# Where the causal mask is added: VectorE in PSUM instead of a TensorE product with a unit matrix

## The chip, the cores and the metric

The kernel runs on one core of one Trainium2 chip. The metric is the device time of one execution in microseconds (us). Before the change three runs took 1765.3, 1765.32 and 1770.0 us; the median is 1765.32 us. The profile is of a further execution.

## The reference, cut to what matters

One decoder layer is computed for a prompt of 1024 tokens and for 8 sample tokens. The change touches only the prompt's attention, with 8 heads and two softmax maps per head:

```python
s = jnp.einsum('bqhcd,bkhcd->bhcqk', q, k).astype(jnp.float32) * (HEAD_DIM ** -0.5)   # c: the two maps
s = jnp.where(mask[None, None, None], s, NEG_INF)        # causal: key position <= query position
p = jax.nn.softmax(s, axis=-1)
a = p[:, :, 0] - lam * p[:, :, 1]
return jnp.einsum('bhqk,bkhe->bqhe', a.astype(v.dtype), v)
```

Queries come in 8 blocks of 128. Block i needs the keys of blocks 0 to i, and only its last score block, the one on the diagonal, has masked places. The rest of the layer (projections, pooling branch, sample attention, gates, MLP) is as it was.

## The kernel before

All products are float32 values split into a high and a low part, three matmuls for each product (L707, L731, L800, L1035, L1097). The program is one instruction stream per engine, written out by hand, with a semaphore for each hand-over. The stages in order of time are: the normed input and the first projection (to about 65 us), eight heads of attention (65 to 552 us), the pooling and sample branches with their projections (to about 1050 us), and the MLP.

**One head on TensorE.** `head(h, par, proj, normed)` (L806) runs steps s = 0 to 8. A step has, in this order: `scores(h, par, s)` (L719), `values(h, par, s-2)` (L758), the first half of the projection of the next head for token tile s (`project`, L681, the matmuls of L707), `weight_transposes` of query block s-1 (L738, L754), the second half of the projection, and `qk_transposes` of the next head for tile s-1 (L716, L717). The last head has no next one, so nothing is projected in it. In steps 0 to 7 `scores` makes the score rows of one query block for both maps c, in PSUM tensor `bank_s` (two banks for each map), in matmuls that contract over 64 rows (L731). At its end two matmuls (L735), one for each map, multiply a bf16 unit matrix by the bf16 mask, and accumulate it on the diagonal block. Their ends raise the semaphore `s_s`.

**The same head on VectorE** (L1596). A step has `maximum` for map 0 and for map 1 (L1554: a wait for `s_s`, the row maximum L1558, the bias L1561), `o_sum` (L1586), `weight_low` (L1580), `weights` (L1568 to L1573), `rotate` (L1543 to L1547, its last instruction raises `s_zfree`, the leave for the next projection to overwrite its bank) and `qk_low` (L1551). In step 1 `normed_head` stands behind the maxima, with a wait for GpSimd's square root (L2152). ScalarE's step is the two exponentials (L1160, each waits for its bias), then `o_out` (L1173), which `o_sum` waits for, then `weight_high` (L1167), which `weight_low` waits for, then the squares, and the copies of the rotated q, k and v.

**What TensorE waits for in a head.** `scores(s)` waits for the exponentials of step s-1 (`s_exp`), as they read the same banks. `values(s-2)` waits for `weight_low` of that block (`s_atlo`). `project(h+1, s, 0)` waits for an earlier `rotate` (`s_zfree`, with the count of `z_before`, L368): of tile 0 in step 2, of tile s-1 in steps 3 to 7, and in step 0 of tile 8 of the head before. `qk_transposes` waits from tile 4 on for `weight_low` (`s_atlo`).

Of the kernel before, what the change touches and what calls it, by code (L numbers as in the profile page):

```python
# [5 lines left out]
ALU = mybir.AluOpType  # L6
# [4 lines left out]
BF16 = mybir.dt.bfloat16  # L11

P = 128
# [63 lines left out]
def decoder_layer(nc, ins, outs):  # L77
# [18 lines left out]
    def put(name, shape, dtype, at=None):  # L96
        size = 1
        for n in shape[1:]:
            size *= n
        size *= 2 if dtype == BF16 else 4  # L100
        off = cursor[0] if at is None else at
        t = nc.alloc_sbuf_tensor_at(name, shape, dtype, offset=off)
        end = (off + size + 31) // 32 * 32
        if at is None:
            cursor[0] = end
        return t, end

    ident, _ = put("ident", [P, P], F32)
    identb, _ = put("identb", [P, P], BF16)
    mask, _ = put("mask", [P, P], BF16)  # L110
    stat, _ = put("stat", [P, 64], F32)
    cols, _ = put("cols", [P, 32], F32)
    nlam, _ = put("nlam", [P, 1], F32)
    half_neg, _ = put("half_neg", [P, 64], F32)
    ones, _ = put("ones", [P, P], F32)
    pages, _ = put("pages", [1, DEC * PAGES], mybir.dt.int32)
    base_h = cursor[0]
    h_hi, _ = put("h_hi", [P, KT, TOK], F32R)
    h_lo, _ = put("h_lo", [P, KT, TOK], F32R)
    w_raw, _ = put("w_raw", [P, 3, KT, P], F32)  # L120
    w_hi, _ = put("w_hi", [P, 3, KT, P], F32R)
    w_lo, _ = put("w_lo", [P, 3, KT, P], F32R)
# [3 lines left out]
    kv_st, _ = put("kv_st", [P, 2, NTT + 1, 2, P], F32)  # L126
    qs_st, _ = put("qs_st", [P, 2, P], F32)
    q_nat, _ = put("q_nat", [P, P], F32)
    qk_hi, _ = put("qk_hi", [P, 2, 2, SEQ], F32R)
    qk_lo, _ = put("qk_lo", [P, 2, 2, SEQ], F32R)  # L130
    v_hl, _ = put("v_hl", [P, 2, NTT, 2, P], F32R)
    rope_c, _ = put("rope_c", [P, NTT + 1, HD], F32)
    rope_s, _ = put("rope_s", [P, NTT + 1, HD], F32)
    rc, _ = put("rc", [P, 2 * P], F32)
    rs, _ = put("rs", [P, 2 * P], F32)
    sums, _ = put("sums", [P, NTT, 2], F32)
    rsum, _ = put("rsum", [P, NTT, 2], F32)
    mx, _ = put("mx", [P, 2, 2], F32)
    nbias, _ = put("nbias", [P, 2, 2], F32)
    ratio, _ = put("ratio", [P, 2], F32)  # L140
    ssq, _ = put("ssq", [P, 2, NTT], F32)
    o_var, _ = put("o_var", [P, NTT], F32)
    o_rstd, _ = put("o_rstd", [P, NTT], F32)
    junk, _ = put("junk", [P, P], F32)
    o_low, _ = put("o_low", [P, P], F32)
    over = cursor[0]
    prob, _ = put("prob", [P, 2, 2, SEQ], F32)
    aT_hi, _ = put("aT_hi", [P, SEQ], F32R)
    aT_lo, _ = put("aT_lo", [P, SEQ], F32R)
    o_st, _ = put("o_st", [P, 2, NTT, P], F32)  # L150
    oT_st, _ = put("oT_st", [P, SEQ], F32, (nc.sbuf_usable_end - 4 * SEQ) // 32 * 32)
# [8 lines left out]
    mask_in, a = put("mask_in", [P, P], F32, a)  # L160
# [6 lines left out]
    kv_slots, _ = put("kv_pages", [P, 2, HEADS // 2 * TOK], F32, r2)  # L167
    kv_pg = kv_slots[:, :, 0:PAGES * D].rearrange("p s (g d) -> p s g d", g=PAGES)
    o_raw, _ = put("o_raw", [P, HEADS, TOK], F32, r2)
    o_lo, _ = put("o_lo", [P, HEADS, TOK], F32R, r2)  # L170
    x1, _ = put("x1", [P, KT, TOK], F32, r2)
# [7 lines left out]
    merged, _ = put("merged", [P, KT, TOK], F32, r3)  # L179
    gx, _ = put("gx", [P, KT, TOK], F32, r3)  # L180
    ff_lo, a = put("ff_lo", [P, KH, TOK], F32R, r3)
    ff_hi, _ = put("ff_hi", [P, KH, TOK], F32R, a)
    ff_raw, _ = put("ff_raw", [P, KH, TOK], F32, r3)
# [3 lines left out]
    smp_q, _ = put("smp_q", [P, D], F32, tmp)  # L187
    smp_k, _ = put("smp_k", [P, D], F32, r4 - 4 * D)
    smp_v, _ = put("smp_v", [P, D], F32, r4 + 2 * NG * TOK * 4 - 4 * TOK)
    ga_sig, _ = put("ga_sig", [P, KT, TOK], F32, r4)  # L190
    o_hi = nc.alloc_sbuf_tensor_at("o_hi", [P, HEADS, TOK], F32R, offset=base_h + full)
    mg_hi = nc.alloc_sbuf_tensor_at("mg_hi", [P, KT, TOK], F32R, offset=base_h)
    mg_lo, _ = put("mg_lo", [P, KT, TOK], F32R, r4)
# [8 lines left out]
    h_smp, _ = put("h_samples", [P, KT, LOW_ROW + DEC], F32R, a)  # L202
# [6 lines left out]
    z_smp, _ = put("z_smp", [P, 3 * P], F32, a)  # L209
# [14 lines left out]
    x_smp, _ = put("x_smp", [P, D], F32, slot2[0])  # L224
# [4 lines left out]
    sq_sum, _ = put("sq_sum", [P, TOK], F32, tmp)  # L229
    diag, a = put("diag", [P, NTT + 1, P], F32, a)  # L230
    assert a <= nc.sbuf_usable_end
    r_bc, _ = put("r_bc", [P, TOK], F32, tmp)
# [45 lines left out]
    with ExitStack() as ctx:  # L278
# [6 lines left out]
        def sem(name):  # L285
            return ctx.enter_context(nc.semaphore(name))
# [37 lines left out]
                                                                  "sample_exp")]  # L324
        s_sela, s_vout, s_v, s_osq, s_oss, s_osv, s_osr, s_osmp = [sem(n) for n in (
            "sel_weights", "v_out", "v_ready", "os_steps", "os_sum", "os_var", "os_rstd", "os_ready")]
        s_hread = sem("h_low_read")
        s_ohi, s_olo, s_addm, s_mghi, s_mglo = [sem(n) for n in ("o_hi", "o_lo", "merged_added", "mg_hi", "mg_lo")]
        s_xt, s_xc, s_sqr, s_sqs = sem("xT_ready"), sem("xT_out"), sem("x1_squares"), sem("squares_added")
        s_n2, s_v2, s_r2 = [sem(n) for n in ("n2_sum", "n2_var", "n2_rstd")]  # L330
# [337 lines left out]
        def _(pe):  # L668
# [50 lines left out]
            def scores(h, par, i):  # L719

                pe.wait_ge(s_qklo, 8 * h + i + 1)
                need(pe, s_exp, 16 * h + 2 * i)
                if i == 4 and h < HEADS - 1:
                    pe.wait_ge(s_zfree, z_before(h + 1, NTT))
                diag = i // 4
                for b in range(1 + diag):
                    n = min(512, (i + 1) * P - 512 * b)
                    for m, (q, k) in enumerate(((qk_hi, qk_hi), (qk_lo, qk_hi), (qk_hi, qk_lo))):
                        for c in range(2):
                            part = slice(HD * c, HD * c + HD)  # L730
                            pe.matmul(bank_s[:, c, 512 * b:512 * b + n], q[part, par, 0, i * P:(i + 1) * P],  # L731
                                      k[part, par, 1, 512 * b:512 * b + n], start=(m == 0),
                                      stop=(m == 2))
                for c in range(2):
                    pe.matmul(bank_s[:, c, i * P:(i + 1) * P], identb[:], mask[:], start=False, stop=True,  # L735
                              skip_group_check=True).then_inc(s_s, 1)

            def weight_transposes(h, i, r, proj):  # L738

# [118 lines left out]
            for t in range(NTT + 2):  # L858
# [6 lines left out]
                if t >= 2:  # L865
                    need(pe, s_qklo, t - 3)
                    qk_transposes(0, 0, t - 2, bank_t[t % 2])
            pe.wait_ge(s_mask, 1)
            head(0, 0, True, False)
            for p in range(0, HEADS // 2 - 1):  # L870
                head(2 * p + 1, 1, True, True)
# [625 lines left out]
        def _(dve):  # L1497
# [56 lines left out]
            def maximum(h, i, c):  # L1554
                n = (i + 1) * P
                k = 16 * h + 2 * i + c + 1
                dve.wait_ge(s_s, k)
                dve.tensor_reduce(mx[:, i % 2, c:c + 1], bank_s[:, c, 0:n], AX_X, ALU.max).then_inc(s_mx, 1)  # L1558
                dve.wait_ge(s_mx, k)
                need(dve, s_exp, k - 4)  # L1560
                dve.tensor_scalar(nbias[:, i % 2, c:c + 1], mx[:, i % 2, c:c + 1], -SCALE, None,  # L1561
                                  ALU.mult).then_inc(s_nb, 1)
# [33 lines left out]
            def head(h, par, proj, normed, k_par):  # L1596
                if proj:
                    split_qkv(h + 1, (2, 3) if normed else (0, 1, 2, 3))
                for s in range(NTT + 1):
                    if s < NTT:  # L1600
                        maximum(h, s, 0)
                        maximum(h, s, 1)
                    if normed and s == 1:
                        normed_head(h - 1, 1 - par)
                    if s >= 2:
                        o_sum(h, par, s - 2)
                    elif s == 0 and normed:
                        o_sum(h - 1, 1 - par, NTT - 1)
                    if s >= 1:
                        weight_low(h, s - 1, 0)  # L1610
                    if s >= 5:
                        weight_low(h, s - 1, 1)
                    if s < NTT:
                        weights(h, s)
                    if s == NTT and h < HEADS - 2:
                        split_qkv(h + 2, (0, 1))
                    if proj:
                        rotate(h + 1, 1 - par, s, k_par)
                    if proj and s >= 1:
                        qk_low(h + 1, 1 - par, s - 1)  # L1620

            def lambda_steps():

                dve.wait_ge(s_const, N_CONST)
                dve.tensor_copy(mask[:], mask_in[:])
                dve.tensor_copy(identb[:], ident[:]).then_inc(s_mask, 1)
                dve.tensor_tensor(lam_pr[:], lam_in[:, 0:4:2], lam_in[:, 1:4:2], ALU.mult).then_inc(s_lam_pr, 1)
                dve.wait_ge(s_lam_pr, 1)
                dve.tensor_reduce(stat[:, 32:34], lam_pr[:], AX_X, ALU.add).then_inc(s_lam_sum, 1)
# [14 lines left out]
            for t in range(NTT + 5):  # L1644
# [20 lines left out]
                if t == NTT + 3:  # L1665
                    lambda_ready()
            dve.wait_ge(s_lam, 1)
            head(0, 0, True, False, 0)
            for p in range(0, HEADS // 2 - 1):
                head(2 * p + 1, 1, True, True, p + 1)  # L1670
# [562 lines left out]
```

## Time and profile before

| | |
|---|---|
| median of 3 runs | 1765.32 us |
| profiled execution, its own time | 1771.14 us |
| its span, first to last instruction | 1769.1 us |
| TensorE matmul busy | 1713.0 us (97%) |
| VectorE busy | 1057.6 us (60%) |
| ScalarE busy | 671.3 us (38%) |
| mean granted TensorE clock | 0.989 of 2.4 GHz |

The span is cut into engine instructions with their start, duration and operands; L735 is line 735 of the kernel. "Idle before" is time in which the engine did nothing ahead of an instruction, with the instruction on another engine whose end released it. TensorE's matmuls are pipelined: the distance from start to start is what one costs in a stream, and the duration also holds the time to run out.

### The profile page before, as it was taken

What the parts mean: (1) busy time and instruction counts of PE and PEld (TensorE: products, weight loads), DVE (VectorE), ACT (ScalarE), POOL (GpSimd) and SP (SyncE); (2) the same over time, 40 slices, a digit from 0 to 9 for tenths busy, and PEclk for the clock granted to TensorE, in tenths of its full rate; (3) what the DMA queues carried; (4) which work ended last, traced back from release to release, by engine and by line L of the source; (5) the groups of instructions that cost most, each with busy time, mean ns of one, the idle gap of its engine ahead of it and who ended that gap; (6) DMA issues with size and microseconds to landing.
All of it is one profiled execution on the core that took longest, in us unless ns stands there. A gap on an engine that the chain in (4) does not pass through costs nothing.

```text
span 1769.1 us, 29201 instructions
## 1 busy us (share of the span) xinstructions
PE 1713.0 (97%) x11756; PEld 1658.1 (94%) x11756; DVE 1057.6 (60%) x1725; ACT 671.3 (38%) x1417; POOL 136.4 (8%) x244
## 2 busy tenths in 40 slices
PE   6999999999977999999999999999999999999997
PEld 6889889888967999999999999999999999999997
DVE  5677777777764788764344457363636363646454
ACT  4355555555544222354312445141414141314132
POOL 3212221221210000000000000000000000000001
PEclk9999999999979999999999999999999999999999
DMA  6202201220220637575222221111111120202112
GB/s 189 70 2 72 73 26 48 73 61 13 73 65 12 224 107 242 171 242 178 93 60 79 65 73 48 49 49 48 49 48 61 36 72 25 72 26 71 48 37 97
DMA packets 136526, 139.13 MB, mean 79 GB/s; under 512 B 6721, under 2 KB 114177, under 8 KB 136384
## 3 DMA queue, kind: packets, MB, share of 16 engines
q1 hardware_dynamic: 135239, 133.07, 24.4%
q10 hardware_dynamic: 1152, 4.19, 0.6%
q8 instruction: 94, 1.54, 0.4%
q14 instruction: 41, 0.33, 0.1%
HBM read 120.29 MB, written 17.18 MB: 78 GB/s over the span
## 4 chain that ended last, share of the span: by engine, by line
PE 90%; DVE 5%; issue 2%; ACT 2%; DMA 1%; SPq 0%; POOL 0%; DVEq 0%; ACTq 0%
PE ps L800 23%; PE ps L1097 21%; PE ps L1035 18%; PE ps L707 16%; PE ps L731 3%; PE ps L764 3%; PE ps L754 1%; PE ps L935 1%; DVE kv_pages L1739 1%; DMA w_raw<-in_w_in 1%; PE ps L735 1%; DVE w_lo L1502 1%; DVE mx L1558 1%; PE ps L773 0%; DVE y_st L2114 0%
## 5 line engine op out<-in xcount | busy, mean ns | idle before, releaser
L2024 DVE TENSOR_TENSOR x<-ps,x 128x1032 f32<-128x1032 f32 x64 | 78.9, 1233 | 223.4 <-PE ps L1097 223.4
L707 PE MATMUL ps<-w_hi,h_hi 128*128 128x384 f32 x520 | 182.6, 351 | 5.8 <-DVE w_lo L1502 3.7
L707 PE MATMUL ps<-w_hi,h_lo 128*128 128x384 f32 x520 | 177.0, 340 | 0.0
L707 PE MATMUL ps<-w_lo,h_hi 128*128 128x384 f32 x520 | 176.5, 339 | 0.0
L1097 PE MATMUL ps<-ff_lo,m_hi 128*128 128x344 f32 x768 | 162.9, 321 | 0.0
L1097 PE MATMUL ps<-ff_hi,m_lo 128*128 128x344 f32 x768 | 162.4, 320 | 0.0
L1097 PE MATMUL ps<-ff_hi,m_hi 128*128 128x344 f32 x768 | 162.1, 319 | 0.0
L1097 PEld LDWEIGHTS ps<-ff_lo,m_hi 128*128 128x128 f32 x768 | 129.1, 188 | 0.0
L1160 ACT ACTIVATE prob<-ps,nbias 128x256 f32<-128x256 f32 (+7 forms) x128 | 95.0, 742 | 88.9 <-DVE nbias L1561 86.5
L1097 PEld LDWEIGHTS ps<-ff_hi,m_hi 128*128 128x128 f32 x768 | 128.3, 188 | 0.0
L1097 PEld LDWEIGHTS ps<-ff_hi,m_lo 128*128 128x128 f32 x768 | 128.2, 188 | 0.0
L1362 ACT ACTIVATE m_hi<-m_down 128x512 fp32r<-128x512 f32 x64 | 40.3, 630 | 215.5 <-PE ps L1097 187.9
L800 PE MATMUL ps<-h_hi,w_hi 128*128 128x344 f32 x480 | 103.3, 324 | 6.4 <-DVE w_lo L1680 3.1
L1035 PE MATMUL ps<-t_hi,m_hi 128*128 128x258 f32 x512 | 104.4, 286 | 2.6 <-ACT part_p L1426 2.6
L707 PEld LDWEIGHTS ps<-w_hi,h_hi 128*128 128x128 f32 x520 | 97.9, 188 | 8.5 <-issue 4.3
L1035 PE MATMUL ps<-t_lo,m_hi 128*128 128x258 f32 x512 | 104.3, 285 | 0.0
L1035 PE MATMUL ps<-t_hi,m_lo 128*128 128x258 f32 x512 | 104.1, 285 | 0.0
L800 PE MATMUL ps<-h_lo,w_hi 128*128 128x344 f32 x480 | 101.8, 320 | 0.0
L800 PE MATMUL ps<-h_hi,w_lo 128*128 128x344 f32 x480 | 101.3, 319 | 0.0
L1558 DVE TENSOR_REDUCE mx<-ps 128x1 f32<-128x256 f32 (+7 forms) x128 | 96.0, 750 | 7.1 <-PE ps L735 6.9
L707 PEld LDWEIGHTS ps<-w_lo,h_hi 128*128 128x128 f32 x520 | 98.3, 189 | 0.6
L707 PEld LDWEIGHTS ps<-w_hi,h_lo 128*128 128x128 f32 x520 | 98.0, 188 | 0.7
(274 smaller groups left out, 3910.4 us busy)
## 6 DMA issues: line engine op xcount, KB each, us to landing
w_raw<-in_w_in SPq DMA_DIRECT2D x44, 512.0 KB, 5.3
kv_pages<-in_cache_k SPq DMA_DIRECT2D x32, 512.0 KB, 5.4
kv_pages<-in_cache_v SPq DMA_DIRECT2D x32, 512.0 KB, 4.9
m_pair<-in_w_up SPq DMA_DIRECT2D x16, 1024.0 KB, 5.5
m_down<-in_w_down SPq DMA_DIRECT2D x16, 1024.0 KB, 5.0
out<-kv_st SPq DMA_DIRECT2D x16, 512.0 KB
x_in<-in_x_prompt SPq DMA_DIRECT2D x8, 512.0 KB, 5.1
attention_out_scratch<-oT_st ACTq DMA_DIRECT2D x8, 512.0 KB, 2.6
```

The source lines that it names most:

```text
L707: mm = pe.matmul(bank[0:n, 0:3 * P], a[:, kt, toks(t)], w[:, :, kt, :], start=(kt == 0 and m == 0), stop=(kt == KT - 1 and m == 2))
L731: pe.matmul(bank_s[:, c, 512 * b:512 * b + n], q[part, par, 0, i * P:(i + 1) * P], k[part, par, 1, 512 * b:512 * b + n], start=(m == 0), s ...
L735: pe.matmul(bank_s[:, c, i * P:(i + 1) * P], identb[:], mask[:], start=False, stop=True, skip_group_check=True).then_inc(s_s, 1)
L754: mm = pe.transpose(bank_t[r][:, (k - 4 * r) * P:(k - 4 * r + 1) * P], prob[:, i % 2, 0, k * P:(k + 1) * P], ident[:])
L764: mm = pe.matmul(bank_o[:, 0:2 * P], a[:, k * P:(k + 1) * P], v_hl[:, par, k].rearrange("p s e -> p (s e)"), start=(k == 0 and m == 0), st ...
L800: mm = pe.matmul(ps[:, SET[sp] + c, 0:CH], w, a[:, c * CH:(c + 1) * CH], start=(first and m == 0), stop=(last and m == 2))
L1035: mm = pe.matmul(acc[:, c], w[:, kt], a[:, kt % kts, c * CW:(c + 1) * CW], start=(opens and kt == 0 and m == 0), stop=(kt == KH - 1 and m ...
L1097: mm = pe.matmul(ps[:, SET[n % 2] + c, 0:CH], w[:, kt], a[:, kt, c * CH:(c + 1) * CH], start=(kt == 0 and m == 0), stop=(kt == KH - 1 and ...
L1160: act.activation(prob[:, i % 2, c, 0:n], bank_s[:, c, 0:n], ACT.Exp, bias=nbias[:, i % 2, c:c + 1], scale=SCALE, accum_out=sums[:, i, c:c ...
L1362: act.activation(ring[k % 3][0][:], weight_source(k), ACT.Copy).then_inc(s_mhi, 1)
L1558: dve.tensor_reduce(mx[:, i % 2, c:c + 1], bank_s[:, c, 0:n], AX_X, ALU.max).then_inc(s_mx, 1)
L2024: dve.tensor_tensor(x1_chunks[:, n], psum_set(n % 2), x1_chunks[:, n], ALU.add).then_inc(s_xadd, 1)
```

## The change

The two mask matmuls of each `scores` go, and with them the bf16 unit matrix `identb`. Instead the last product of the diagonal's bank raises `s_s`, and VectorE adds the bf16 mask to the diagonal block in PSUM, in place, ahead of each row maximum. The maximum waits on a new semaphore `s_msk` for that add. There are 128 matmuls fewer and 128 VectorE instructions more (8 heads, 8 query blocks, 2 maps). VectorE instead of TensorE waits for the mask to be ready.

```diff
-    identb, _ = put("identb", [P, P], BF16)
...
                         for c in range(2):
                             part = slice(HD * c, HD * c + HD)
-                            pe.matmul(bank_s[:, c, 512 * b:512 * b + n], q[part, par, 0, i * P:(i + 1) * P],
-                                      k[part, par, 1, 512 * b:512 * b + n], start=(m == 0),
-                                      stop=(m == 2))
-                for c in range(2):
-                    pe.matmul(bank_s[:, c, i * P:(i + 1) * P], identb[:], mask[:], start=False, stop=True,
-                              skip_group_check=True).then_inc(s_s, 1)
+                            mm = pe.matmul(bank_s[:, c, 512 * b:512 * b + n], q[part, par, 0, i * P:(i + 1) * P],
+                                           k[part, par, 1, 512 * b:512 * b + n], start=(m == 0),
+                                           stop=(m == 2))
+                            if b == diag and m == 2:
+                                mm.then_inc(s_s, 1)
...
-            pe.wait_ge(s_mask, 1)
             head(0, 0, True, False)
...
                 k = 16 * h + 2 * i + c + 1
                 dve.wait_ge(s_s, k)
+                diag = bank_s[:, c, i * P:(i + 1) * P]
+                dve.tensor_tensor(diag, diag, mask[:], ALU.add).then_inc(s_msk, 1)
+                dve.wait_ge(s_msk, k)
                 dve.tensor_reduce(mx[:, i % 2, c:c + 1], bank_s[:, c, 0:n], AX_X, ALU.max).then_inc(s_mx, 1)
...
-                dve.tensor_copy(mask[:], mask_in[:])
-                dve.tensor_copy(identb[:], ident[:]).then_inc(s_mask, 1)
+                dve.tensor_copy(mask[:], mask_in[:]).then_inc(s_mask, 1)
...
             dve.wait_ge(s_lam, 1)
+            dve.wait_ge(s_mask, 1)
             head(0, 0, True, False, 0)
```

## Rows read from the trace of the kernel before

**Rows 1.** The page's chain that ended last, shares by engine.

```profile
PE 90%; DVE 5%; issue 2%; ACT 2%; DMA 1%; SPq 0%; POOL 0%; DVEq 0%; ACTq 0%
```

**Rows 2.** Busy time by stretch: head 3, last head. From:to, length, busy us, clock.

```profile
core 0: us, PE busy (x) PEld busy (x) DVE busy (x) ACT busy (x) POOL busy (x), PEclk, DMA share, GB/s
253.30:316.05 62.75, 62.22 (x430) 56.48 (x428) 47.27 (x119) 33.15 (x92) 14.77 (x27) 1.00 0.19 52
504.40:552.00 47.60, 29.06 (x185) 22.36 (x184) 32.12 (x77) 23.60 (x65) 4.89 (x3) 0.78 0.21 61
```

**Rows 3.** Timeline, TensorE, around one mask pair. Start us, us, instruction [idle before].

```profile
280.96 0.28 PE L731 MATMUL ps<-qk_lo,qk_hi 64*128 64x128 f32 x2
281.17 0.28 PE L735 MATMUL ps<-mask,identb 128*128 128x128 bf16 x2
281.26 0.36 PE L764 MATMUL ps<-v_hl,aT_hi 128*128 128x256 f32 x1
281.46 0.28 PE L764 MATMUL ps<-v_hl,aT_lo 128*128 128x256 f32 x1
281.58 0.28 PE L764 MATMUL ps<-v_hl,aT_hi 128*128 128x256 f32 x1
```

**Rows 4.** Timeline, VectorE, a 128x128 subtraction out of PSUM, and the maxima of step 4.

```profile
266.92 0.28 DVE L1580 TENSOR_TENSOR aT_lo<-ps,aT_hi 128x128 fp32r<-128x128 f32 x1
...
281.43 0.82 DVE L1558 TENSOR_REDUCE mx<-ps 128x1 f32<-128x640 f32 x1 [0.71 <-PE ps L735]
282.29 0.16 DVE L1561 TENSOR_SCALAR nbias<-mx 128x1 f32<-128x1 f32 x1
282.36 0.81 DVE L1558 TENSOR_REDUCE mx<-ps 128x1 f32<-128x640 f32 x1
```

**Rows 5.** Timeline, VectorE, head 3: what hands over to TensorE, and its idle time.

```profile
256.85 0.21 DVE L1547 COPY kv_st<-z_smp 8x128 f32<-8x128 f32 x1
...
273.81 0.28 DVE L1547 COPY kv_st<-ps 128x128 f32<-128x128 f32 x1
...
285.43 0.69 DVE L1580 TENSOR_TENSOR aT_lo<-ps,aT_hi 128x512 fp32r<-128x512 f32 x1 [0.50 <-ACT aT_hi L1167]
...
292.76 0.89 DVE L1580 TENSOR_TENSOR aT_lo<-ps,aT_hi 128x512 fp32r<-128x512 f32 x2 [0.35 <-ACT aT_hi L1167]
...
300.62 1.02 DVE L1580 TENSOR_TENSOR aT_lo<-ps,aT_hi 128x512 fp32r<-128x512 f32 x2 [0.23 <-ACT aT_hi L1167]
...
303.74 0.28 DVE L1547 COPY kv_st<-ps 128x128 f32<-128x128 f32 x1
...
309.01 1.16 DVE L1580 TENSOR_TENSOR aT_lo<-ps,aT_hi 128x512 fp32r<-128x512 f32 x2
...
314.43 0.35 DVE L1586 SCALAR_TENSOR_TENSOR o_st<-ps,rsum,o_low 128x128 f32<-128x128 f32 x1 [1.42 <-ACT o_low L1173]
315.10 1.29 DVE L1580 TENSOR_TENSOR aT_lo<-ps,aT_hi 128x512 fp32r<-128x512 f32 x2 [0.32 <-ACT aT_hi L1167]
```

**Rows 6.** Timeline, TensorE, head 3: the instructions that wait for those of VectorE.

```profile
257.11 0.44 PE L707 MATMUL ps<-w_hi,h_hi 128*128 128x384 f32 x1 [0.35 <-DVE kv_st L1547]
...
267.66 0.36 PE L764 MATMUL ps<-v_hl,aT_hi 128*128 128x256 f32 x1
...
274.27 0.34 PE L707 MATMUL ps<-w_hi,h_hi 128*128 128x384 f32 x1
...
305.61 0.34 PE L707 MATMUL ps<-w_hi,h_hi 128*128 128x384 f32 x1
...
312.18 0.28 PE L764 MATMUL ps<-v_hl,aT_hi 128*128 128x256 f32 x1
```

**Rows 7.** Waits of head 0. Who waited for whom: us in total, times, longest.

```profile
DVE rc L1543 <- PE ps L707: 4.7, 4, 2.4
```

**Rows 8.** Waits of the last head, same columns.

```profile
PE ps L731 <- ACT prob L1160: 13.3, 6, 3.9
```

**Rows 9.** Timeline, TensorE, head 0: a stall, and a fall of the clock behind it.

```profile
68.26 0.41 PE L707 MATMUL ps<-w_hi,h_hi 128*128 128x384 f32 x1 [2.09 <-DVE w_lo L1502]
...
69.63 0.53 PE L707 MATMUL ps<-w_lo,h_hi 128*128 128x384 f32 x1
69.95 0.53 PE L707 MATMUL ps<-w_hi,h_lo 128*128 128x384 f32 x1
```

More of the change, by code:

```diff
@@ L326, in decoder_layer @@
             "sel_weights", "v_out", "v_ready", "os_steps", "os_sum", "os_var", "os_rstd", "os_ready")]
-        s_hread = sem("h_low_read")
+        s_hread, s_msk = sem("h_low_read"), sem("scores_masked")
         s_ohi, s_olo, s_addm, s_mghi, s_mglo = [sem(n) for n in ("o_hi", "o_lo", "merged_added", "mg_hi", "mg_lo")]
```

## The prediction

> **What bounds the kernel now.** I read the page's chain of waits first: 90% of it is TensorE, 5% VectorE [rows 1]. That is a mean over stages, so I cut the span by head. In head 3 TensorE is busy 62.22 of 62.75 us and VectorE 47.27 [rows 2]; heads 1 to 6 (six stretches of equal length) show the same to 0.1 us. In the last head, which has no projection beside it, TensorE is busy 29.06 of 47.60 us and VectorE 32.12: no engine fills it, it is a chain from engine to engine. The sum of busy times would leave VectorE 15 us of room in each of heads 1 to 6. Whether it is room is seen only in the timeline, by setting each TensorE instruction that waits for VectorE beside the VectorE instruction that releases it [rows 5, 6]. There the margins are small: the projection of step 3 starts at 274.27, and the copy that frees its bank ends at 273.81 + 0.28 = 274.09; the value product of step 2 starts at 267.66, its operand is ready at 266.92 + 0.28 = 267.20 [rows 4 to 6]. At the head's start TensorE already waits for VectorE (0.35 us at 257.11). So in these heads TensorE is the bound by tenths of a microsecond, with VectorE close behind.
>
> **What one mask pair gives back on TensorE.** From the start of the pair (281.17) to the second value product (281.46) are 0.29 us for two mask matmuls and one value product; the next value product stands 0.12 behind [rows 3]. So a pair costs m = 0.29 - 0.12 = 0.17 us. The last score pair starts at 280.96 and needs 0.11, so 0.10 us more lie ahead of the mask pair, where TensorE goes from 64 rows to 128. I leave that in: the product behind takes 128 rows too. Its bounds are 0 and 0.10 a pair. Heads 0 to 6 have 56 pairs, 9.5 us if TensorE stayed the bound. In the last head the saving mostly lies beside the chain.
>
> **What one add puts on VectorE.** The trace has no VectorE write into PSUM. The nearest row is the 128x128 subtraction with one operand in PSUM and one in SBUF, 0.28 us [rows 4]. The maximum must wait for the add; a dependent pair stands 0.04 apart (281.43 + 0.82 = 282.25 to 282.29). I take x = 0.32 us for an add, 0.64 for a step. Lower bound: an independent pair overlaps by 0.09 (282.29 + 0.16 = 282.45 against 282.36), so x = 0.28 - 0.09 = 0.19, say 0.20. Upper bound: the dearest 128x128 operation, 0.35 for L1586 [rows 5], plus 0.04, x = 0.39. In a head there are 16 adds, 5.1 us; what counts is where this lateness meets TensorE.
>
> The Trainium skill bears on the wait (VectorE: DVE Perf Modes, "The DRAIN you can't avoid"): the next operation starts only when the pipeline is empty, with or without a semaphore, so that the semaphore "costs nothing extra". By that an add would cost only the distance between two neighbours. Here the trace shows 0.13 us between a dependent and an independent pair, which speaks against it.
>
> **The walk through head 3**, times of before, shifts against them. It starts at 257.11, where TensorE starts on VectorE's copy that ends at 257.06 [rows 5, 6], a hand-over of 0.05. D is how late VectorE is, P how late TensorE is.
> - Steps 0 and 1: four adds, D = 1.28. VectorE is busy or waits for followers of its own biases (ScalarE, GpSimd), so all of it stays. The operand of the value product is ready at 267.20 + 1.28 + 0.05 = 268.53; TensorE, two mask pairs shorter, is there at 267.66 - 0.34 = 267.32. A new stall of 1.2 us, P = +0.87.
> - Step 2: D = 1.92. Bank free for the projection of step 3 at 274.09 + 1.92 + 0.05 = 276.06; TensorE is there at 274.27 + 0.87 - 0.17 = 274.97. A second stall of 1.1 us, P = +1.79.
> - Step 3: D would be 2.56, but VectorE had 0.71 us to wait for the scores of step 4 [rows 4]. These now come at 280.96 + 0.28 + 1.79 = 283.03 against 281.43: D = 1.60 at step 4's first maximum.
> - Steps 4 to 6: +0.64 each. The waits before L1580 shrink from 0.50 through 0.35 and 0.23 to none [rows 5]. What stands over the 0.13 that ScalarE itself takes is time for TensorE's transposes, and a late VectorE doesn't pay it: -0.37, -0.22, -0.10. D = 1.87, 2.29, 2.83. Bank free for the projection of step 7 at 303.74 + 0.28 + 2.83 + 0.05 = 306.90; TensorE, four pairs on, is there at 305.61 + 1.79 - 0.68 = 306.72. P = +1.29.
> - Step 7: D = 3.47. Value product of step 8: 309.01 + 1.16 + 3.47 + 0.05 = 313.69 against 312.18 + 1.29 = 313.47. P = +1.51.
> - Step 8 has no maximum. VectorE had 1.42 us to wait before L1586 [rows 5], so D = 2.05 there. L1580 stood 0.67 behind, 0.32 of it a wait that goes; with nothing to wait for it stands 0.35 - 0.09 = 0.26 behind (the overlap above), and D = 2.05 + 0.26 - 0.67 = 1.64. TensorE's next transposes and the copy that starts the next head hang on that.
>
> So a head of this kind becomes about 1.6 us longer; the 1.4 us that eight pairs give back are in this already. Six such heads: 9.6 us. What hides the rest of the 5.1 us is the 0.71 before the scores of step 4, the 1.42 in step 8 and the transposes' share.
>
> **Head 0** has more room: VectorE waits there 4.7 us in four waits for the projection [rows 7]. The same walk with these waits taken off ends within 0.2 us of none: about one us of stall in steps 7 and 8 against the mask pairs saved. I take 0, bounds -1.2 (eight pairs, the first of which stands ahead of a wait anyway) and +0.8.
>
> **The last head** is the chain maximum, exponential, next scores. TensorE waits 13.3 us in six waits for exponentials [rows 8]. All 16 adds stand in that chain: 16 x 0.32 = 5.1 us. In one step (4) the chain runs through the scores and gives a pair back, 0.2 to 0.3. I take +4.9. From its end on TensorE is the bound again and nothing can take this back: VectorE's load there doesn't change.
>
> **Sum.** 9.6 + 0 + 4.9 = +14.5 us on the profiled execution, 1771.1 to 1785.6. That execution stands 5.8 us above the median, which differs only by what varies from run to run, so the median goes from 1765.3 to 1779.8, say 1780. The two copies that prepared the mask run in the first stage under TensorE's projections; one of them going is nothing. All SBUF buffers move down 256 bytes, which I cost at nothing: no row reads otherwise by place. TensorE's 128 instructions less are in m.
>
> **The same walk at the bounds.** x = 0.39: stalls at the same four places, P = 2.2 after step 3, 2.6 at the end; 6 x 2.6 + 0.5 + 6.0 = +22, 1787. x = 0.20: P = 1.07 after step 3, 0.4 in step 7, 0.3 at the end; 6 x 0.3 - 1 + 3.0 = +4, 1769.
>
> **Rivals.**
> 1. TensorE stays the bound. VectorE is busy only 75% of such a head [rows 2], and an add that cost next to nothing would leave the margins whole. Heads 0 to 6 then give back 9.5 us, with the 0.10 ahead of the pair 15.1, against at most 5 in the last head: 1755 to 1761. Against it stand the margins of 0.46 and 0.18 us [rows 4 to 6]. It decides from an x under about 0.15, and no VectorE row of 128 elements is that short.
> 2. The wait for the add is free and the add overlaps its neighbour, x = 0.20: +4, 1769, within what can be told. The rule of the Trainium skill named above would lead here. The 0.04 after the end of the instruction waited for speaks against.
> 3. Writing PSUM is dearer than reading it, x = 0.39 or more: 1787 to 1792. Nothing in the trace is for or against.
> 4. The clock falls. In head 0 a stall of 2.09 us is followed by matmuls that take 0.53 instead of 0.34 us and stand 0.32 instead of 0.17 apart, from 69.4 to 72.8 us, at 1.2 instead of 2.4 GHz [rows 9]. That costs 10 x 0.145 = 1.5 us. The new stalls of steps 2 and 3 are 1.2 and 1.1 us; if each head paid one such stretch, 7 to 10 us more, 1787 to 1790. In its favour: they are near each other, and the stalls of the last head grow by 0.6 each. Against: the clock is 1.00 over head 3 with its stalls of 0.4 us.
>
> **How the numbers follow.** The forecast (x of 0.27 to 0.36, +10 to +18) gets 62%, rival 1 7% (4 below -0.3%, 3 within), rival 2 7%, rival 3 12%, rival 4 12%. A change of 0.3%, 5.3 us, is about what a measurement of this kernel can tell from none. Slower: 62 + 12 + 12 = 86%; the same: 10%; faster: 4%. The likeliest time is 1780, its own range 1775 to 1784. For 8 in 10 I add rivals 3 and 4 up to 1790 and go down to 1770, just above rival 2.
>
> **What would show it.** After the change the mask pair is missing and the value product follows the scores 0.17 sooner. An add shows about 0.28 us with the maximum 0.04 behind. Head 3 is 64.3 us instead of 62.75, with VectorE busy about 51.8. TensorE waits about 1.2 us before L764 of step 2 for VectorE's L1580, and about 1.1 before the projection of step 3 for the copy L1547. The last head is 4.9 longer. The prediction is wrong if the period of a head falls below 62.7 (then VectorE had room), if an add is far from 0.28, or if the granted clock of heads 1 to 6 falls under 1.00.

## The result, and the profile after

| | before | after |
|---|---|---|
| median, runs side by side | 1766.4 us (1765.3 to 1770.0, 4 runs) | 1794.56 us (1793.62 to 1795.89, 4 runs) |
| profiled execution, its own time | 1771.14 us | 1793.62 us |
| its span | 1769.1 us | 1791.6 us |
| TensorE matmul busy | 1713.0 us (97%) | 1715.9 us (96%) |
| VectorE busy | 1057.6 us (60%) | 1092.1 us (61%) |

The ratio is 1.014, with a 95% interval of 1.0122 to 1.0157: slower, as forecast, but by 28 us on the medians and 22.5 us on the two profiled executions, where I had said 14.5. The time lies 4.6 us above the range. Later runs of the same kernel before gave a median of 1770.39 us (15 runs, 1765.14 to 1772.82) and of 1769.67 us (7 runs), so 1765.3 was the low end of what it does by itself. The kernel after was not run beside these; set against their medians its 1794.56 would be 24 to 25 us more, which is an estimate. The interval of 1.2 to 1.6% is clear of no change.

The page after: first the busy times, then the chain that ended last, shares by engine.

```profile
PE 1715.9 (96%) x11628; PEld 1653.4 (92%) x11628; DVE 1092.1 (61%) x1852; ACT 669.5 (37%) x1417; POOL 136.4 (8%) x244
...
PE 70%; DVE 18%; issue 6%; ACT 3%; DMA 1%; SPq 1%; POOL 1%; ACTq 0%; DVEq 0%
```

The busy shares have hardly moved. The chain has: VectorE had 5% of it [rows 1] and has 18%. By busy time TensorE still looks like the only bound of this program; by the chain VectorE now shares that place in the heads. The next two rows are head 3 and the last head after (from:to, length, busy us, clock), as in [rows 2].

```profile
263.45:329.41 65.96, 62.73 (x413) 55.72 (x413) 51.61 (x135) 32.80 (x91) 14.77 (x27) 1.00 0.17 49
525.31:575.24 49.93, 29.64 (x157) 23.94 (x156) 36.45 (x92) 22.79 (x63) 4.89 (x3) 0.73 0.19 58
```

Head 3 takes 65.96 us where it took 62.75. All six heads of this kind do the same: the instruction that ends each (VectorE's `z_smp`) stands at 130.02, 195.99, 261.94, 327.89, 393.83, 459.77 and 525.31, 65.95 apart (the last 65.54), against 62.76 before (the last 62.36). For the last head I take the same stretch in both, from `z_smp` to the first product of the stage behind it: 45.81 us before, 49.93 after. The 22.5 us between the two profiled executions are then:

| stretch | forecast | measured |
|---|---|---|
| start, up to 68 us | 0 | -0.1 |
| head 0 | 0 | 0.1 (1.6 without the clock, below) |
| heads 1 to 6 | 6 x 1.6 = 9.6 | 6 x 3.19 = 19.1 |
| last head | 4.9 | 49.93 - 45.81 = 4.1 |
| the rest | 0 | -0.7 |

The add itself is as forecast. The next two lines are its group (busy us, mean ns, idle before and releaser) and its place in step 7's maximum on VectorE's timeline.

```profile
L1556 DVE TENSOR_TENSOR ps<-ps,mask 128x128 f32<-128x128 f32 x128 | 37.1, 290 | 3.2 <-PE ps L730 3.2
```

```profile
313.44 0.29 DVE L1556 TENSOR_TENSOR ps<-ps,mask 128x128 f32<-128x128 f32 x1
313.76 1.22 DVE L1558 TENSOR_REDUCE mx<-ps 128x1 f32<-128x1024 f32 x1
```

From 313.44 to 313.76 are 0.32, so x is 0.32 to 0.33 and a step costs 0.65 (I had 0.64). Not the price of the operation was wrong, but where it is paid. TensorE's timeline over head 3 shows each wait that is left (last column: idle before, releaser):

```profile
263.45 0.45 PE L706 MATMUL ps<-w_hi,h_hi 128*128 128x384 f32 x1 [0.42 <-DVE kv_st L1544]
274.66 0.39 PE L762 MATMUL ps<-v_hl,aT_hi 128*128 128x256 f32 x1 [0.73 <-DVE aT_lo L1580]
282.22 0.45 PE L706 MATMUL ps<-w_hi,h_hi 128*128 128x384 f32 x1 [0.83 <-DVE kv_st L1544]
310.87 0.33 PE L715 MATMUL ps<-ident,q_nat 128*128 128x128 f32 x1 [0.44 <-DVE aT_lo L1580]
320.06 0.33 PE L715 MATMUL ps<-ident,q_nat 128*128 128x128 f32 x1 [0.59 <-DVE aT_lo L1580]
325.99 0.33 PE L715 MATMUL ps<-ident,q_nat 128*128 128x128 f32 x1 [0.17 <-DVE aT_lo L1580]
329.41 0.44 PE L706 MATMUL ps<-w_hi,h_hi 128*128 128x384 f32 x1 [0.42 <-DVE kv_st L1544]
```

The second and the third are the two stalls that I forecast. The forecast's other two, the projection of step 7 and the value product of step 8, aren't there. In their place stand two that it doesn't name, at 310.87 and 320.06: the transposes of the next head's q and k (`qk_transposes`, L715 here), in steps 6 and 7, which wait for `weight_low` (L1580). This is VectorE's side of it:

```profile
301.38 0.89 DVE L1580 TENSOR_TENSOR aT_lo<-ps,aT_hi 128x512 fp32r<-128x512 f32 x2
...
309.80 1.02 DVE L1580 TENSOR_TENSOR aT_lo<-ps,aT_hi 128x512 fp32r<-128x512 f32 x2
...
318.85 1.16 DVE L1580 TENSOR_TENSOR aT_lo<-ps,aT_hi 128x512 fp32r<-128x512 f32 x2
```

They end at 302.27, 310.82 and 320.01, and the three transposes start at 302.32, 310.87 and 320.06, each 0.05 behind. (The first of them shows no idle time, since the matmul before it is still running out.) In the trace of before the same three transposes, of steps 5, 6 and 7, start without a wait. Their `weight_low` ends at 292.76 + 0.89 = 293.65, 300.62 + 1.02 = 301.64 and 309.01 + 1.16 = 310.17 [rows 5]:

```profile
294.13 0.27 PE L716 MATMUL ps<-ident,q_nat 128*128 128x128 f32 x1
...
302.10 0.27 PE L716 MATMUL ps<-ident,q_nat 128*128 128x128 f32 x1
...
310.57 0.27 PE L716 MATMUL ps<-ident,q_nat 128*128 128x128 f32 x1
```

Over attention's heads this wait went from 1.2 to 8.7 us; the lines are the waits before, then after (us in total, times, longest):

```profile
PE ps L716 <- DVE aT_lo L1580: 1.2, 7, 0.2
```

```profile
PE ps L715 <- DVE aT_lo L1580: 8.7, 22, 0.6
```

The line was in the trace of before, with 0.2 at most a time, always in step 8; that it had a margin of 0.40 to 0.48 in three other steps doesn't show in a list of waits.

### The profile page after: what moved, and what is told of

The parts are those of the page before. It is cut to its first block, busy times and chain, and to the rows that moved or that the text cites. A ratio compares the mean times of both kernels' runs of the same rounds, so it can differ in the third digit from the quotient of the medians.

```text
span 1791.6 us, 29071 instructions
## 1 busy us (share of the span) xinstructions
PE 1715.9 (96%) x11628; PEld 1653.4 (92%) x11628; DVE 1092.1 (61%) x1852; ACT 669.5 (37%) x1417; POOL 136.4 (8%) x244
## 4 chain that ended last, share of the span: by engine, by line
PE 70%; DVE 18%; issue 6%; ACT 3%; DMA 1%; SPq 1%; POOL 1%; ACTq 0%; DVEq 0%
PE ps L798 22%; PE ps L1094 20%; PE ps L1032 18%; DVE mx L1558 5%; PE ps L706 4%; DVE aT_lo L1580 2%; DVE ps L1556 1%; DVE w_lo L1499 1%; DVE rc L1540 1%; DMA w_raw<-in_w_in 1%; ACT aT_hi L1164 1%; DVE nbias L1561 1%; DVE rs L1542 1%; PE ps L762 1%; PE ps L932 1%
```

## The experiments

Before them I walked head 3 once more with that wait put in. It gave a head of +3.2 us, which is what had been measured, so it was fitted to it: it needed a test. Theory A is this walk; its rival B is the walk of the prediction, with the missing cost somewhere else, for example in an add that costs VectorE more than its own time.

**The kernel before, once more**, to see what varies by itself.

> The kernel before, unchanged, profiled once more. The profiled execution shown ahead of the prediction took 1771.1 us, its median 1766.4. Theory A: the difference is chance in TensorE's clock. Then a second profile shows heads 1 to 6 again at 62.75 us each and differs only in stretches at the lower clock level in head 0 and the last head (some 1.5 us each), with a time of 1765 to 1771. Rival B: the heads themselves vary; then their period moves by 0.1 us or more and all sums made from one profile are that uncertain.

Measured: 1766.83 us, span 1764.7, clock 0.992, a head 62.77 us. The heads are constant, three other stretches are not. TensorE's first projection of attention starts at 66.38 instead of 68.26. Head 0 from there on and the last head differ by their clock. The windows of these two stretches, first in the execution shown of before, then in this one (columns as in [rows 2]):

```profile
68.26:130.08 61.82, 61.65 (x412) 56.11 (x413) 44.82 (x112) 30.66 (x86) 10.37 (x24) 0.97 0.16 44
506.24:552.05 45.81, 27.39 (x173) 21.10 (x171) 31.84 (x76) 22.65 (x63) 4.89 (x3) 0.78 0.21 63
```

```profile
66.38:126.69 60.31, 60.14 (x412) 54.58 (x413) 44.73 (x111) 30.66 (x86) 10.36 (x24) 1.00 0.16 45
502.87:547.25 44.38, 25.56 (x173) 19.66 (x171) 31.85 (x76) 22.66 (x63) 4.89 (x3) 0.85 0.22 65
```

VectorE and ScalarE are busy for the same time to a tenth, TensorE for 1.5 and 1.8 us less at a higher granted clock. Start-up gives 1.9 us, the two clocks 1.5 and 1.4, and the later stages take 0.4 back: 4.4 us of span between two executions of one kernel. The low stretch of head 0 [rows 9] isn't there in the second one:

```profile
66.38 0.41 PE L707 MATMUL ps<-w_hi,h_hi 128*128 128x384 f32 x1 [2.09 <-DVE w_lo L1502]
66.63 0.34 PE L707 MATMUL ps<-w_lo,h_hi 128*128 128x384 f32 x1
66.81 0.34 PE L707 MATMUL ps<-w_hi,h_lo 128*128 128x384 f32 x1
```

The stall is the same 2.09 us, and the matmuls behind it stay at 0.34. After the change the stall is 2.31 and they stay at 0.34 too, so its head 0 of 61.88 has to be set against 60.31: +1.6 us, not +0.1. That head's waits are again those of the transposes (0.20, 0.44 and 0.57 us in steps 5 to 7).

**No mask anywhere**: the most that taking it from TensorE can bring.

```diff
-                diag = bank_s[:, c, i * P:(i + 1) * P]
-                dve.tensor_tensor(diag, diag, mask[:], ALU.add).then_inc(s_msk, 1)
-                dve.wait_ge(s_msk, k)
```

> The mask is added nowhere: the two mask matmuls are gone, and the add and its wait on VectorE are left out too, so that the weights of later keys are not suppressed. It measures the saving on TensorE alone. Theory A, the corrected walk with every hand-over: heads 1 to 6 give back only 0.6 to 0.8 us each and not 1.4, as VectorE's copy for the projection of step 3 and its subtraction for the turned q and k of step 7 come no earlier; the last head gives back about 2 us (eight pairs in its chain). In all -5 to -8 us against the kernel before, 1758 to 1761. Rival B, as recorded: eight pairs of 0.17 us a head in full, 9.5 us, with the last head -11.5, 1755. Rival C, the 0.10 us ahead of the pair goes too: 1749 or less.

Measured: 1765.66 us against 1770.39, ratio 0.9977 (0.9965 to 0.9989), a head 62.45 us. The prize is 0.31 us a head, a fifth of the 1.4 that I had put into the prediction for eight pairs, and below the 0.6 expected here too. The whole is 4.7 us faster, just short of the 5 expected; heads 1 to 6 are 1.9 of it, and the rest lies in stretches that vary from run to run by as much. TensorE's timeline at the change from the last scores to the value product:

```profile
277.40 0.28 PE L730 MATMUL ps<-qk_lo,qk_hi 64*128 64x128 f32 x2
277.61 0.39 PE L762 MATMUL ps<-v_hl,aT_hi 128*128 128x256 f32 x1
277.83 0.28 PE L762 MATMUL ps<-v_hl,aT_lo 128*128 128x256 f32 x1
```

From the last score pair to the second value product are 0.43 us here and 0.50 with the mask pair between them (280.96 to 281.46, [rows 3]). A pair therefore cost m = 0.07, not 0.17. The first value product behind the change from 64 to 128 rows takes 0.22 until the next one, also without a mask pair, where the later ones take 0.12; I had taken it at 0.12 and put the tenth down to the mask. The Trainium skill has a rule that would be the reason, "Mode switching requires drain" (TensorEngine Tiling (Array Packing), Key Properties); the trace agrees that a change of the rows costs, and puts it at a tenth ahead of the first product of 128 rows and a tenth behind it, but doesn't show a drain as such.

Eight pairs of 0.07 would be 0.56 us a head. Of the first four nothing is left: in step 3 TensorE's projection starts at 270.62 in this run, 0.06 behind the end of VectorE's copy, which comes no earlier than before. From there on each missing pair puts TensorE 0.07 ahead (its transposes of the next head's q and k stand 0.09, 0.16, 0.23 and 0.30 us earlier in steps 4 to 7), and this is the 0.31.

**Adds on VectorE, with TensorE's mask products kept**: the loss without the prize. (The mask is added twice in it.)

```diff
                 dve.wait_ge(s_s, k)
+                diag = bank_s[:, c, i * P:(i + 1) * P]
+                dve.tensor_tensor(diag, diag, mask[:], ALU.add).then_inc(s_msk, 1)
+                dve.wait_ge(s_msk, k)
```

> The kernel before with the adds of the change put on VectorE as well, TensorE's mask matmuls kept (the mask is added twice, which leaves the weights as they are). It measures what the adds alone cost. Theory A: the adds are the whole of the loss, and in heads 1 to 6 VectorE's chain is the bound, so that TensorE's saving is worth next to nothing: heads at 65.9 to 66.3 us, in all +28 to +33 us against the kernel before, of which up to 2 are mask matmuls in the chain of the last head. Rival B: TensorE's saving counts in full beside the adds; then this is 9.5 + 2 us dearer than the changed kernel, 1806. Rival C: the loss comes from something else in the change (the moved buffers, the earlier semaphore); then this is near the kernel before.

Measured: 1798.64 us, ratio 1.0161 (1.0145 to 1.0176), a head 66.13 us, the last head 51.30. Theory A's range holds (28.3 us over the kernel before), B's 1806 and C fall. The adds are the whole loss, and as the buffers lie here as in the kernel before, their move isn't needed for it. Removing a head's 16 mask products brings 0.18 us when VectorE sets the pace (65.95 against 66.13).

**The transposes a step later.** In the kernel after, `qk_transposes` of tiles 4 to 6 are issued in the next step, behind its scores, and VectorE's `qk_low` behind its maxima:

```diff
                     scores(h, par, s)
+                    if proj and s >= 6: turn_qk(s - 2)
...
-                    if s >= 1: turn_qk(s - 1)
+                    if s >= 1 and s not in (5, 6, 7): turn_qk(s - 1)
```

> The changed kernel with one order moved: in steps 5 to 7 the transposes of the next head's q and k (tiles 4, 5 and 6) are issued in the step that follows, behind its scores, and VectorE's low part of them behind its maxima. They wait for the low part of the transposed weights, which the recorded walk left out. Theory A: that missing wait is what made a head 3.2 us longer and not 1.6. Then heads 1 to 6 fall from 65.96 to 64.4 us, and the whole from 1794.6 to about 1785. Rival B: VectorE's own chain sets the length of a head whatever TensorE waits for in it; then nothing changes, 1794.

Measured: 1792.55 us, ratio 1.0136 (1.0121 to 1.0152), a head 65.27 us: 0.7 better than after, of the 1.5 expected. It neither bears A out nor refutes it, since the edit didn't take the waits away but exchanged them; that nothing changes, as B said, isn't so either. On TensorE's timeline the two stalls of 0.44 and 0.59 are gone, and three others stand there:

```profile
305.18 0.44 PE L752 MATMUL ps<-ident,prob 128*128 128x128 f32 x2 [0.15 <-DVE qk_lo L1552]
...
313.80 0.44 PE L752 MATMUL ps<-ident,prob 128*128 128x128 f32 x2 [0.15 <-DVE qk_lo L1552]
...
316.64 0.33 PE L715 MATMUL ps<-ident,q_nat 128*128 128x128 f32 x1 [0.21 <-DVE aT_lo L1584]
```

The weight transposes now wait for `qk_lo`, as both share a bank, and the transposes of tile 6, ahead of step 8's projection, still come before `weight_low` is done. A cleaner test leaves the order alone and moves the lateness:

**Adds for blocks 0 to 3 only, and for blocks 4 to 7 only**; the other blocks keep their mask products.

```diff
+        def on_dve(i):
+            return i < 4        # the other kernel: i >= 4
...
+                            if on_dve(i) and b == diag and m == 2:
+                                mm.then_inc(s_s, 1)
...
                 for c in range(2):
-                    pe.matmul(bank_s[:, c, i * P:(i + 1) * P], identb[:], mask[:], ...)
+                    if not on_dve(i):
+                        pe.matmul(bank_s[:, c, i * P:(i + 1) * P], identb[:], mask[:], ...)
```

> VectorE adds the mask in query blocks 0 to 3 of each head only; in blocks 4 to 7 TensorE's mask matmuls stay. Theory A, the walk of all hand-overs (an add costs 0.33 us, a mask pair gives back 0.07): lateness on VectorE meets TensorE at the value product of step 2 (+0.65) and the projection of step 3 (+1.6), and nothing is added behind; heads 1 to 6 get a period of 64.3 to 64.4 us instead of 62.76. Rival B, the recorded walk: the same 1.6, as the wait it left out lies in later steps. This run alone does not tell them apart, the next one does.

> The other half: VectorE adds the mask in query blocks 4 to 7 only, TensorE's mask matmuls stay in blocks 0 to 3. Theory A: the lateness meets the transposes of the next head's q and k in steps 5 to 7, which wait for the low part of the transposed weights with 0.35 to 0.43 us of margin: +0.3 in step 5, +0.9 in step 6, +1.6 in step 7. Heads 1 to 6 get 64.3 to 64.5 us. Rival B, the recorded walk without that wait: all other hand-overs have over 1.4 us of margin, the heads get 62.8 to 63.0 us. If A holds, the halves sum to the 3.2 us a head of the whole change.

Measured, early: 1781.16 us against 1769.67, ratio 1.0063 (1.0046 to 1.008), a head 64.52 us, a tenth over the 64.3 to 64.4 expected. Late: 1782.38 us, ratio 1.0071 (1.0053 to 1.0088), a head 64.20 us, where A had said 64.3 to 64.5 and the recorded walk 62.8 to 63.0. These are all of TensorE's waits of head 3 between its first projection and step 8, early and then late:

```profile
269.76 0.38 PE L772 MATMUL ps<-v_hl,aT_hi 128*128 128x256 f32 x1 [0.73 <-DVE aT_lo L1592]
277.32 0.45 PE L712 MATMUL ps<-w_hi,h_hi 128*128 128x384 f32 x1 [0.85 <-DVE kv_st L1555]
```

```profile
304.75 0.33 PE L721 MATMUL ps<-ident,q_nat 128*128 128x128 f32 x1 [0.43 <-DVE aT_lo L1592]
313.94 0.33 PE L721 MATMUL ps<-ident,q_nat 128*128 128x128 f32 x1 [0.59 <-DVE aT_lo L1592]
```

Each half has its own two of the four stalls of the kernel after, to 0.02 us. Over a head they cost +1.76 and +1.44, together 3.20, against 3.19 for the whole change. So the early adds are lost in steps 2 and 3, as forecast, the late ones at the transposes of steps 5 to 7, and B falls.

**One add for both maps** in blocks 2 to 7 (256 columns instead of twice 128).

```diff
+                if i < 2 or c == 0:
+                    dve.wait_ge(s_s, k if i < 2 else k + 1)
+                    maps = slice(c, c + 1) if i < 2 else slice(0, 2)
+                    diag = bank_s[:, maps, i * P:(i + 1) * P]
+                    dve.tensor_tensor(diag, diag, to_add, ALU.add).then_inc(s_msk, 1)
```

> The changed kernel with one add for both maps (256 columns) instead of two in query blocks 2 to 7; the maximum of map 0 then waits for the scores of both maps, which end together. Theory A: the step's adds cost 0.46 us instead of 0.67, VectorE's lateness shrinks by 0.2 a step, and heads 1 to 6 fall from 65.95 to 64.9 us; with the last head 1.2 shorter the whole falls by about 7.5 us against the changed kernel. Rival B: the number of adds doesn't matter, only their columns; then the heads stay at 65.9.

Measured: 1785.75 us, ratio 1.0088 (1.0071 to 1.0105), a head 64.93 us as expected. The wide add takes 0.43 us in the mean, so with its wait it saves 0.2 a step.

**Each add twice** (the mask is added twice).

```diff
+                for twice in range(2):
                     dve.tensor_tensor(diag, diag, mask[:], ALU.add).then_inc(s_msk, 1)
+                    dve.wait_ge(s_msk, 2 * (k - 1) + twice + 1)
```

> The changed kernel with every add done twice, one behind the other with a wait between (the mask is added twice, which leaves the weights as they are). Theory A: the first 5.3 us of adds a head cost 3.2, as 2 us of them went into waits that VectorE had; these are used up, so the second 5.3 us cost 5.2 in each of heads 1 to 6: 71.1 us a head, in the last head 5.3 more, in all about +42 us against the changed kernel, 1836. Rival B: the cost is in proportion to the adds; then a head is 3.2 longer again, 69.2 us, in all about 1821.

Measured: 1839.21 us, ratio 1.0385 (1.0364 to 1.0405), the heads by turns 71.31 and 72.15 us, in the mean 71.7, 0.6 over A's value and 2.5 over B's. The windows of heads 3 and 4 (columns as in [rows 2]) show where the alternation comes from:

```profile
277.60:348.90 71.30, 62.97 (x415) 55.81 (x413) 56.38 (x151) 32.87 (x92) 14.76 (x27) 1.00 0.16 45
348.90:421.05 72.15, 64.36 (x415) 57.40 (x414) 56.50 (x152) 32.91 (x92) 14.74 (x27) 0.98 0.16 45
```

It is the clock. In step 3 both heads have the same stall of 1.10 us, behind one of 1.7 in step 2. In head 3 the matmuls behind it take 0.34 us, in head 4 0.53, at 1.2 GHz from 371.2 to 374.7:

```profile
299.87 0.44 PE L706 MATMUL ps<-w_hi,h_hi 128*128 128x384 f32 x1 [1.10 <-DVE kv_st L1544]
300.15 0.34 PE L706 MATMUL ps<-w_lo,h_hi 128*128 128x384 f32 x1
300.33 0.34 PE L706 MATMUL ps<-w_hi,h_lo 128*128 128x384 f32 x1
...
371.18 0.51 PE L706 MATMUL ps<-w_hi,h_hi 128*128 128x384 f32 x1 [1.10 <-DVE kv_st L1544]
371.48 0.53 PE L706 MATMUL ps<-w_lo,h_hi 128*128 128x384 f32 x1
371.80 0.53 PE L706 MATMUL ps<-w_hi,h_lo 128*128 128x384 f32 x1
```

In a head at full clock the second 16 adds, some 5.3 us of VectorE, cost 71.31 - 65.95 = 5.4 where the first 16 cost 3.2: the slack of before is used up, as A says. The 0.84 us of every other head is the price of the clock.

None of the versions that add the mask is faster than the kernel before. With the other instructions in this order, the kernel without a mask shows the most that another placing could bring: 0.3 us a head.

## Why the prediction was wrong

- *"TensorE is the bound by tenths of a microsecond, with VectorE close behind"*: right. It is what made the change a loss at all, and the busy shares (97% and 60%) said the contrary.
- *x = 0.32 for an add*: right, 0.32 to 0.33. The Trainium skill's rule by which the wait is free (rival 2; VectorE: DVE Perf Modes, "The DRAIN you can't avoid") doesn't hold here: the maximum starts 0.03 us behind the end of the add that it waits for (313.44 + 0.29 to 313.76). Its formula for a float32 `tensor_tensor`, (N + 151)/0.96 ns (VectorE: DVE Perf Modes, the section on the TRN2 errata), gives an estimate of 291 ns for 128 columns, though it is measured there for other sizes; the mean of 290 ns of the add in PSUM agrees.
- *VectorE's walk*: right to 0.03 us from step 4 on. D at step 4's maximum was forecast +1.60 and is 289.37 - 6.34 - 281.43 = +1.60 (6.34 is the distance between the two heads' starts, 257.11 and 263.45); for `weight_low` of steps 4 to 7 forecast +1.87, +2.29, +2.83, +3.47, measured +1.90, +2.28, +2.84, +3.50. Before that VectorE is 0.2 us less late than forecast: +1.06 instead of +1.28 at the subtraction of step 2, +1.73 instead of +1.92 at the copy (274.32 - 6.34 - 266.92 and 281.88 - 6.34 - 273.81). `o_var` (L1591) takes 0.16 us in step 1 where it took 0.44 in heads 1 to 6 of before; the runs don't show why. So "all of it stays" didn't hold there. That +1.60 at step 4's maximum came out to the hundredth is in part luck: TensorE starts step 3's projection only 1.61 us late and not 1.79, but loses a tenth again behind the stall (the second matmul starts at 282.50, 0.28 behind the first, where it was 0.18 before), so that its last score pair is 289.06 - 6.34 - 280.96 = 1.76 late.
- *Stalls of steps 2 and 3, P = +0.87 and +1.79*: right in place, measured +0.66 and +1.61. The difference is the 0.2 us of VectorE just named. As idle time they show 0.73 and 0.83 us, not the 1.2 and 1.1 that I named as a sign: the 0.2 is missing in the first, TensorE arrived later than forecast as m is 0.07, and a stall's beginning lies under the matmul before it.
- **The step that failed** is *"TensorE, four pairs on, is there at 305.61 + 1.79 - 0.68"* and what follows from it, P = +1.29 and +1.51. Between step 3 and step 7 I let TensorE run free. It doesn't: in steps 5, 6 and 7 `qk_transposes` waits for `weight_low`. I had named this wait in the description of the kernel, and counted it only at the end, in step 8. Before, `weight_low` ended at 293.65, 301.64 and 310.17, and the transposes started at 294.13, 302.10 and 310.57: margins of 0.48, 0.46 and 0.40, about as narrow as the 0.46 of step 2 that I did walk. A D of +2.28, +2.84 and +3.50 less these margins, and 0.05 for the hand-over, give P = +1.85, +2.43 and +3.15. Measured are 302.32 - 6.34 - 294.13 = +1.85, 310.87 - 6.34 - 302.10 = +2.43, and 320.06 - 6.34 - 310.57 = +3.15. From there the shift stays: the value product of step 8 starts at 321.73 - 6.34 - 312.18 = +3.21.
- *"VectorE had 1.42 us to wait before L1586, so D = 2.05 there"*: this followed from the same step. With TensorE 3.2 late the value product comes late as well, so VectorE still waits 1.13 us for its output, and only 0.3 of the 1.42 is caught up: D goes from +3.50 to 323.98 - 6.34 - 314.43 = +3.21. The head's end is +3.2 instead of +1.6.
- *m = 0.17*: too dear, it is 0.07. In the kernel after it made little difference, since VectorE set the pace at each of these waits, but rival 1's times were too good by it: not 1755 to 1761, but at best the 4.7 us of the kernel without a mask.
- *Head 0 at nothing, bounds -1.2 and +0.8*: +1.6 like for like. It has the same waits in steps 5 to 7.
- *The last head, +4.9*: +4.1 on the two profiled executions, +5.5 against the second execution of before, which differs from the first by clock alone. Right within what can be told.
- *Rival 4, the clock*: in heads 1 to 6 it didn't come. Their granted clock is 1.00 with stalls of 0.8 us in each. It wasn't far: with each add done twice, stalls of 1.7 and 1.1 us brought it in every other head, for 0.84 us.
- *The signs of being wrong*: none of the three came (a head under 62.7, an add far from 0.28, a clock under 1.00), and the prediction was wrong all the same. None of them looked for a head longer than forecast.
- *The range* had as its upper end the same walk with x = 0.39, or one clock stretch a head. Both were bounds of sizes, and none was a bound for an omitted wait. The base was also low, by 1 us against the runs side by side and by 4 to 5 against the later medians: I took the median of three runs (1765.3) for the kernel's, where the profiled execution stood 5.8 above it.

## What to carry to other kernels

When work is put on an engine that sets another's pace by tenths of a microsecond, walk every wait of the other engine for it, those too that never wait in the trace: take the list of waits from the code and write a margin (start of the waiter less end of the waited-for) beside each. An engine that is 60% busy over the program, and 75% in these heads, had no room for 5.1 us in a head of 62.8, and lost 3.2 of them; what a second portion of the same size costs (5.4 at full clock) is not what the first cost. And a product that sits at a change of the array's rows is nearly free, because the change is paid without it too: measure the distance across the whole place, not the product's own.

## What the runs showed of the hardware

- VectorE adds a bf16 tile from SBUF to a float32 block of 128x128 in PSUM, in place, in 0.29 us, as long as the subtraction that only reads PSUM (0.28), and 128x256 over two separate banks in 0.43.
- Two bf16 matmuls with the unit matrix between products of 64 and of 128 rows cost 0.07 us together.
- The same kernel with the same stall of TensorE (2.09 us) went on at 1.2 GHz from 69.4 to 72.8 us in one execution, and at 2.4 GHz in another; the kernel after went on at 2.4 GHz behind 2.31 us, the kernel without a mask fell to 1.2 GHz behind the same 2.31 (granted clock 0.83 from 65.77 to 75.77). With each add done twice the stalls of 1.7 and 1.1 us, the same in every head, were followed by 1.2 GHz in every other head only. The stall alone doesn't decide.
